# Two decoder blocks on one core: the turning of seven norms spread into the products around them

## What is computed

```python
def rms_norm(x, g):          # the seven norms before mlp, gate, mixers
    y = x * rsqrt(mean(x * x, axis=-1) + 1e-6)
    return y * g

h = h + mixer(rms_norm(h, ln_mix)) @ w_out
h = h + square(relu(rms_norm(h, ln_mlp) @ w_mlp1)) @ w_mlp2
gate = sigmoid(rms_norm(h, ln_ple) @ w_ple_gate)
h = h + (p @ w_ple_proj) * gate
...
x = x + rms_norm(y, post_norm)   # second decoder, y the mixer's output
```

## Time and profile before

| | us |
|---|---|
| median of 3 runs | 2127.03 (2123.44 to 2127.22) |
| the profiled execution | 2124.92 |
| its span, first to last instruction | 2123.1 |
| TensorE's matmuls busy in it | 2007.9 |
| DVE, ScalarE, GpSimd busy | 1068.2, 896.8, 221.3 |
| mean granted TensorE clock | 0.981 |

### The profile page before, as it was taken

One profiled execution on the slowest core, in us unless ns is written; L12 is line 12 of the kernel. 1 busy time (PEld: TensorE's weight loads), 2 busy tenths in 40 slices (PEclk: granted clock), 3 DMA queues, 4 the chain that ended last, 5 costly groups with the idle time before them and its releaser, 6 DMA issues. The chain is left out here.

```text
span 2123.1 us, 27350 instructions
## 1 busy us (share of the span) xinstructions
PE 2007.9 (95%) x11189; PEld 1614.4 (76%) x11189; DVE 1068.2 (50%) x1706; ACT 896.8 (42%) x1653; POOL 221.3 (10%) x225
## 2 busy tenths in 40 slices
PE   7999889999999899999999999998999899989888
PEld 6778768888887777557888888776887688856567
DVE  5676455343435442674543443446344655355763
ACT  5561354322314543674432232445334532245552
POOL 1020000000000000441000000000000034133440
PEclk9999999999999999999999999998999999999999
DMA  5221113332322123111223332122221156400001
GB/s 154 66 79 42 41 40 109 100 99 99 99 99 81 60 89 100 40 40 60 92 97 99 99 99 99 64 77 94 80 90 41 44 177 177 141 21 29 13 7 64
DMA packets 122481, 169.93 MB, mean 80 GB/s; under 512 B 7482, under 2 KB 83654, under 8 KB 122358
## 3 DMA queue, kind: packets, MB, share of 16 engines
q1 hardware_dynamic: 114502, 150.47, 21.9%
q0 software_dynamic: 5504, 14.58, 2.5%
q10 hardware_dynamic: 2352, 3.15, 0.4%
HBM read 158.22 MB, written 2.10 MB: 76 GB/s over the span
## 5 line engine op out<-in xcount | busy, mean ns | idle before, releaser
L412 DVE TENSOR_TENSOR WL<-RAW,WH 128x1024 fp32r<-128x1024 f32 (+1 forms) x283 | 347.7, 1231 | 376.8 <-ACT WH L482 376.3
L482 ACT CAST WH<-RAW 128x1024 fp32r<-128x1024 f32 (+1 forms) x283 | 293.3, 1038 | 392.8 <-PE PSUM L516 390.4
L516 PE MATMUL PSUM<-XH,WH 128*128 128x512 f32 (+4 forms) x1128 | 422.7, 375 | 7.9 <-DVE XL L412 3.8
L516 PE MATMUL PSUM<-XL,WH 128*128 128x512 f32 (+4 forms) x1128 | 414.8, 368 | 0.0
L516 PE MATMUL PSUM<-XH,WL 128*128 128x512 f32 (+4 forms) x1128 | 414.5, 367 | 0.0
L516 PE MATMUL PSUM<-WH,HP 128*128 128x512 f32 x1024 | 317.9, 390 | 1.9 <-DVE WL L412 1.9
L516 PE MATMUL PSUM<-WH,XH 128*128 128x512 f32 (+1 forms) x608 | 240.5, 396 | 16.6 <-DVE WL L412 10.4
L516 PEld LDWEIGHTS PSUM<-XH,WH 128*128 128x128 f32 (+3 forms) x1128 | 213.4, 189 | 47.1 <-DVE WL L412 4.9
L516 PEld LDWEIGHTS PSUM<-XL,WH 128*128 128x128 f32 (+3 forms) x1128 | 213.4, 189 | 36.8 <-issue 2.9
L516 PEld LDWEIGHTS PSUM<-XH,WL 128*128 128x128 f32 (+3 forms) x1128 | 212.9, 189 | 35.3
L516 PE MATMUL PSUM<-WL,XH 128*128 128x512 f32 (+1 forms) x608 | 233.0, 383 | 0.0
(11 more groups left out here) (236 smaller groups left out, 2489.9 us busy)
## 6 DMA issues: line engine op xcount, KB each, us to landing
RAW<-in_w_mlp_dram SPq DMA_DIRECT2D x64, 1024.0 KB, 5.2
RAW<-in_nsa_w_in_dram SPq DMA_DIRECT2D x14, 1024.0 KB, 5.5
RAW<-in_w_in_e_dram SPq DMA_DIRECT2D x12, 1024.0 KB, 5.3
RAW<-in_w_qkv_o_dram SPq DMA_DIRECT2D x12, 1024.0 KB, 5.2
RAW<-in_gla_w_in_dram SPq DMA_DIRECT2D x12, 1024.0 KB, 5.2
RAW<-in_w_ple_gate_dram SPq DMA_DIRECT2D x8, 1024.0 KB, 5.0
RAW<-in_w_out_e_dram SPq DMA_DIRECT2D x4, 1024.0 KB, 5.0
RAW<-in_w_out_o_dram SPq DMA_DIRECT2D x4, 1024.0 KB, 5.0
```

The costliest lines, as they stand in the source:

```text
L412: return x.do.tensor_tensor(o, a, b, op)
L482: a.do.copy(hi, r).then_inc(*up("w_hi", "w_hi", j))
L516: m = p.do.matmul(o, l, r, start=start and i == 0, stop=stop and i == len(pairs) - 1)
```

## The change

No instruction is added or dropped; the lists of TensorE, ScalarE and DVE are put in another order at seven norms.

- TensorE: in MLP0, MLP1, PLE0 and PLE1 the turns of tiles 0 to 2 stay, that of tile 3 goes behind the first half product (MLP), or behind two tiles of p's first product (PLE). In ODD and GLA tile 0's turn comes after tile 1's products, tile 1's inside tile 3 (after its first part of the tail), tiles 2 and 3 after the first and second half product. In NSA tiles 0 and 1 are both turned inside tile 3, tiles 2 and 3 as in ODD. `pe_turn` can take banks ahead of the ring.
- `dve_turn` is split into `dve_gain` and `dve_rest`, and the new lists `act_norm`, `dve_norm` (MLP and PLE norms) and the written-out ones of ODD, GLA and NSA interleave them with the scales, adds and weights of neighbouring tiles.
- TensorE waits for both halves of XL by name (`x_whole`), and `turns()` follows the new order.

```diff
 def out_norm(i, n):
-                for u in ([t - 1] if t else []) + ([3] if t == 3 else []):
+                for u in {2: (0, 1), 3: (2, 3)}.get(t, ()):
...
+        def x_whole(p, n, t):
+            for h in (1, 0):
+                p.wait_ge(*at("xl", n, t, h))
...
 def toks(...)
+                        if within and n > 1 and i == 0:
+                            within(t)
...
-        def pe_turn(p, n, t):
+        def pe_turn(p, n, t, ahead=None):
             for h in range(2):
                 p.wait_ge(*at("xn", n, t, h))
                 turned(p, ("nt", n, t, h), lambda b: [
...
-                    for c in range(4)])
+                    for c in range(4)], bank=None if ahead is None else (ps.next + ahead + h) % 8)
...
         def pe_ready(p, n, t):
             if t:
                 pe_turn(p, n, t - 1)
-            if t == 3:
-                pe_turn(p, n, 3)
...
+        def act_norm(a, n, j):
+            act_scale(a, n, 0)
+            act_scale(a, n, 1)
+            act_turn(a, n, 0)
+            act_scale(a, n, 2)
+            act_turn(a, n, 1)
+            act_weights(a, j + 2)
+            act_scale(a, n, 3)
+            act_weights(a, j + 3)
+            act_turn(a, n, 2)
+            act_turn(a, n, 3)
+
+        def dve_norm(v, n, j, add):
+            add(0)
+            dve_scale(v, n, 0)
+            add(1)
+            dve_gain(v, n, 0)
+            dve_scale(v, n, 1)
+            dve_rest(v, n, 0)
+            add(2)
+            dve_gain(v, n, 1)
+            dve_scale(v, n, 2)
+            dve_rest(v, n, 1)
+            dve_weights(v, j + 1)
+            add(3)
+            dve_weights(v, j + 2)
+            dve_scale(v, n, 3)
+            dve_gain(v, n, 2)
+            dve_rest(v, n, 2)
+            dve_weights(v, j + 3)
+            dve_gain(v, n, 3)
+            dve_rest(v, n, 3)
...
 def pe_mlp: up_
-                    feats_first(p, [("up", l, 0, m) for m in range(3)], n)
+                    feats_first(p, [("up", l, 0, m) for m in range(3)], n, mid=[lambda: pe_turn(p, n, 3)])
...
 def pe_ple
+            toks(p, ("pv", l, 0), p_ready, 1, "P", (PP[:, 0], PP[:, 1]), after=lambda t: pe_turn(p, n, 3) if t == 1 else None)
+            toks(p, ("pv", l, 1), p_ready, 1, "P", (PP[:, 0], PP[:, 1]))
             toks(p, ("pg", l, 0), normed(n), head=True)
-            toks(p, ("pg", l, 1), normed(n), tail=True, after=after)
+            toks(p, ("pg", l, 1), normed(n), tail=True, after=lambda t: pe_turn(p, n + 1, 0) if t == 1 else None,
+                 within=lambda t: pe_turn(p, n + 1, 1) if t == 3 else None)
...
 def act_ple, second column half of the gate
+            gate(1, 0)
+            act_scale(a, n + 1, 0)
+            gate(1, 1)
+            act_turn(a, n + 1, 0)
+            act_scale(a, n + 1, 1)
+            gate(1, 2)
+            act_weights(a, j + 4)
+            act_turn(a, n + 1, 1)
+            act_weights(a, j + 5)
+            gate(1, 3)
+            act_scale(a, n + 1, 2)
+            act_weights(a, j + 6)
+            act_scale(a, n + 1, 3)
+            act_turn(a, n + 1, 2)
+            act_turn(a, n + 1, 3)
...
 def dve_ple, second column half
+            add(1, 0)
+            dve_scale(v, n + 1, 0)
+            dve_gain(v, n + 1, 0)
+            add(1, 1)
+            dve_scale(v, n + 1, 1)
+            dve_rest(v, n + 1, 0)
+            dve_gain(v, n + 1, 1)
+            dve_weights(v, j + 4)
+            dve_rest(v, n + 1, 1)
+            add(1, 2)
+            add(1, 3)
+            dve_scale(v, n + 1, 2)
+            dve_weights(v, j + 5)
+            dve_gain(v, n + 1, 2)
+            dve_scale(v, n + 1, 3)
+            dve_weights(v, j + 6)
+            dve_rest(v, n + 1, 2)
+            dve_gain(v, n + 1, 3)
+            dve_rest(v, n + 1, 3)
...
 def pe_odd (pe_gla alike)
+            feats_first(p, [("oq", *f) for f in o_feats[:3]], ODD, mid=[lambda: pe_turn(p, ODD, 2, 0), lambda: pe_turn(p, ODD, 3, 2)])
...
 def pe_gla
+            def within(t):
+                if t == 3:
+                    pe_turn(p, NSA, 0)
+                    pe_turn(p, NSA, 1)
+            toks(p, ("yo", 0, 1), gla_ready, tail=True, within=within)
...
 def act_gla
+            out_scale(0)
+            out_scale(1)
+            act_scale(a, NSA, 0)
+            act_scale(a, NSA, 1)
+            out_scale(2)
+            act_turn(a, NSA, 0)
+            act_turn(a, NSA, 1)
+            act_weights(a, j + 4)
+            out_scale(3)
+            act_weights(a, j + 5)
+            act_scale(a, NSA, 2)
+            act_weights(a, j + 6)
+            act_scale(a, NSA, 3)
+            act_turn(a, NSA, 2)
+            act_turn(a, NSA, 3)
...
 def dve_gla
+            dve_out_gain(v, 0, 1, 0)
+            dve_out_add(v, 0, 0)
+            dve_out_gain(v, 0, 1, 1)
+            dve_out_add(v, 0, 1)
+            dve_scale(v, NSA, 0)
+            dve_out_gain(v, 0, 1, 2)
+            dve_scale(v, NSA, 1)
+            dve_gain(v, NSA, 0)
+            dve_gain(v, NSA, 1)
+            dve_out_add(v, 0, 2)
+            dve_rest(v, NSA, 0)
+            dve_rest(v, NSA, 1)
+            dve_weights(v, j + 4)
+            dve_out_gain(v, 0, 1, 3)
+            dve_out_add(v, 0, 3)
+            dve_scale(v, NSA, 2)
+            dve_weights(v, j + 6)
+            dve_gain(v, NSA, 2)
+            dve_scale(v, NSA, 3)
+            dve_rest(v, NSA, 2)
+            dve_gain(v, NSA, 3)
+            dve_rest(v, NSA, 3)
...
 def pe_nsa
+            feats_first(p, [("ns",), ("nq", 0), ("nq", 1)], NSA, "SFF", [lambda: pe_turn(p, NSA, 2), lambda: pe_turn(p, NSA, 3)])
```

More of the change, by code:

```diff
@@ L851, in down, with add @@
                 dve_weights(v, j + (3 if q == 3 and c else 5))
-                for t in range(4):
+                def add(t):
                     o = H[:, t, 512 * c:512 * c + 512]
@@ L855, in down @@
                     tt(v, o, o, bank("down", l, q, c, t)[:, :], ALU.add).then_inc(*ps.read("down", l, q, c, t))
+                if q == 3 and c:
+                    dve_norm(v, n + 1, j + 3, add)
+                    return
+                for t in range(4):
+                    add(t)
                     if q == 3:
[L857 to L860, removed]
+                        dve_half(v, n + 1, t)
                 if q < 3 or c == 0:
@@ L907, in act_ple, with gate @@
                 act_weights(a, first_part["pv", l, c] + 3)
[L908 to L927, removed]
+            def gate(c, t):
+                g = GTE[:, t, 512 * c:512 * c + 512]
+                a.wait_ge(*ps.full("pg", l, c, t))
+                act(a, g, bank("pg", l, c, t)[:, :], ACT.Exp, scale=-1.0).then_inc(*ps.read("pg", l, c, t))
+                a.wait_ge(*ps.free("pg", l, c, t))
+                step(a, act(a, g, g, ACT.Ln, bias=ONEC))
+                act(a, g, g, ACT.Exp, scale=-1.0).then_inc(*up("ple_gate", "ple_gate", l, c, t))
+            j = first_part["pg", l, 0]
+            act_weights(a, j + 5)
+            for t in range(4):
+                gate(0, t)
+                if t:
+                    act_half(a, n + 1, t - 1)
+            act_half(a, n + 1, 3)
+            act_weights(a, j + 6)
+            j = first_part["pg", l, 1]
+            act_weights(a, j + 3)
+            gate(1, 0)
[13 more added lines that the diff above has]
+            act_turn(a, n + 1, 3)
         def dve_ple(v, l):
@@ new lines, in dve_ple @@
+            j = first_part["pg", l, 0]
+            dve_weights(v, j + 5)
+            for t in range(4):
+                add(0, t)
+                if t:
+                    dve_half(v, n + 1, t - 1)
+            dve_half(v, n + 1, 3)
+            dve_weights(v, j + 6)
+            j = first_part["pg", l, 1]
+            dve_weights(v, j + 3)
+            add(1, 0)
[3 more added lines that the diff above has]
+            dve_scale(v, n + 1, 1)
@@ L1723, in round_ @@
                     pv(h)
-            feats_first(p, [("oq", *f) for f in o_feats[:3]], ODD)
+            feats_first(p, [("oq", *f) for f in o_feats[:3]], ODD, mid=[lambda: pe_turn(p, ODD, 2, 0), lambda: pe_turn(p, ODD, 3, 2)])
             for k in range(8):
@@ L1828, in act_odd @@
             act_weights(a, j + 3)
-            for t in range(4):
-                act_ready(a, MLP1, t, j + 3)
+            act_norm(a, MLP1, j + 3)
         def dve_odd(v):
@@ L1915, in dve_odd @@
                     tt(v, o, o, bank("oo", c, t)[:, :], ALU.add).then_inc(*ps.read("oo", c, t))
-                    if c:
-                        dve_ready(v, MLP1, t, j + 3)
-                    else:
+                if c:
+                    dve_norm(v, MLP1, j + 3, add)
+                else:
+                    for t in range(4):
+                        add(t)
                         dve_half(v, MLP1, t)
-                if not c:
                     dve_weights(v, j + 6)
```

123 lines of the change are left out of this document (41 added, 82 removed).

## The result

The changed kernel takes 2098.98 us (median of 4, 2096.64 to 2099.40) against 2125.59 (median of 4, 2123.44 to 2127.22) of the kernel before in the same session: a ratio of 0.9873, 95% interval 0.9856 to 0.9890, some 27 us. The profiled execution took 2099.40 with a span of 2097.2; the span before was 2123.1.

A forecast was written before the change was run, and what follows sets the result against it. TensorE, busy 95% of the span, was taken as the bound. Gains of 2.9 + 4.8 + 3.4 + 5.95 + 5.7 + 7.3 = 30.0 us took 2124.92 to 2094.9; 2.1 for the median gave 2097, range 2089 to 2110.

The forecast's parts named there:

- What bounds: Whole kernel: TensorE binds; at seven norms 33.8 us of XN waits and 14.2 us of low-clock loss.
- MLP1, PLE0, PLE1: Tile 3's turn hidden behind product work at these norms: gains of 2.9, 2.4 and 2.4 us.
- the 0.6 us wait for WL: MLP1's first half product: TensorE waits 0.6 us for the first new weights, instead of 2.03 us at the turn.
- The bank wait foretold at PLE: PLE0 and PLE1: p's second half waits near 0.7 us for its bank, which DVE copies after tile 3's rest.
- MLP0: MLP0 norm: a gain of 3.4 us, with only two parts (2.7 us) covering each tile.
- the term of 2.4 us for the first weight: MLP0: the first weights are there 2.4 us after TensorE has run out of work.
- the 0.7 for a low clock: MLP0: 0.7 us taken off for an even chance that low clock (1.5 us) follows the weight wait.
- ODD and GLA: These two norms: gains of 5.95 and 5.7 us, after new waits of 2.8 and 2.7 us.
- NSA: NSA norm: a gain of 7.3 us, after new waits of 1.3, 3.4 and 0.6 and 1.0 for the clock.
- The GpSimd term: NSA: GpSimd's rests and DVE's work go one after the other, 1.5 us at the first product, 0.5 before second halves.
- the rivals: Whole kernel: queues take half back, 2111, chance 0.14; low clock stays, 2106, 0.10; slower, 0.04; does nothing, 2127, 0.02.
- The rival "slower": First weight work before add 3 or gate 3 waits for its transfer and delays the add; 2131.4 or more, chance 0.04.

The follow-up runs named there:

- the run with filled waits: The kernel before, no turn moved, with 17 to 56 transposes that nobody reads in each of TensorE's waits at the norms: 2117.39 us.
- the banks mended: The changed kernel with tile 2's turn in MLP1 given a bank other than the one holding tile 3's product: 2090.31 us.
- The undone halves: The changed kernel, in MLP and PLE norms, with ScalarE's and DVE's old order (2109.56 us), or with tile 3's turn ahead of the first products again (2113.56 us).
- The later turn: The changed kernel with tile 0's turn in ODD and GLA within tile 2's product instead of ahead of it: 2098.40 us.
- The five runs with banks: The changed kernel with NSA banks 2088.14, MLP1 banks 2090.31, both 2087.87, ring set ahead of nz 0 2093.50; the kernel before with that ring line 2122.81 us.
- the old lists: The changed kernel with ScalarE's and DVE's lists in the MLP and PLE norms back in their old order: 2109.56 us.
- two programs: The changed kernel with all bank edits and NSA's low halves on DVE: 2080.91 us; the same plus 26 unread transposes before NSA's first product: 2085.28 us.

## Why the prediction was right, and where it was not

The time was forecast at 2097 and is 2098.98; the range holds it. The gain was forecast at 30.0 us and is 26.6 by the medians of one session, 25.9 in the traces. That it is so near is in part luck, since errors met: the seven norms gave 2.6 more than foretold and other places 2.4, and 9.2 were lost where the prediction did not look.

- **What bounds**: right. The XN waits fell from 33.8 to 7.2 us (7 expected), and the run with filled waits shows the clock's part to be real, at 11.4 us of the 14.2 claimed (one of NSA's waits stayed unfilled).
- **MLP1, PLE0, PLE1**: 2.4, 2.6, 2.6 for 2.9, 2.4, 2.4. In MLP1 the 0.6 us wait for WL did not come; a bank wait of 1.17 came in its place (with the banks mended the wait for WL is there, 0.43). The sum took the weights as the only thing that could hold TensorE and did not follow the ring. The bank wait foretold at PLE is there and smaller (0.36 for 0.6). The undone halves show that turns and lists are both needed.
- **MLP0**: the term of 2.4 us for the first weight was wrong. TensorE waited 0.79 us there, for XL. DVE had split two weight tiles in one go at 296.18, as it had at 296.38 in the kernel before; the tail uses up only two parts, so one of the first product's weights was ready long before. The row was there to read, and the sum had gone by the rule of the other norms. With the 0.7 for a low clock that did not follow, that makes 2.3 of the 2.6 us missed.
- **ODD and GLA**: the waits came at the places and sizes foretold: 1.56 and 1.53 for 1.5, 0.61 for 0.7, 0.32 and 1.23 for 0.6 and 1.2. ODD got 0.9 more, since the low clock that had followed a wait for weights near 720 was absent. The later turn shows that the 1.5 us are not the turn's fault, which the sum had charged to it.
- **NSA**: 1.00 for 1.3, 3.23 for 3.4, 0.24 for 0.6; 6.5 us for 7.3, since the low clock behind the 3.23 cost more than 1.0 (6.8 us of it). The GpSimd term was of the right kind: in NSA DVE's sum of 1024 columns and its two subtractions took 1.2 us more beside GpSimd at the first product, for the 1.5 of the sum. The page "SBUF — State Buffer" of the Trainium skill, section "SBUF: two separate sides", has the pair of ports locked for the whole of an instruction. The trace agrees: DVE's first subtraction, begun at 1662.83, took 1.75 us, until 0.54 behind the end of GpSimd's at 1664.03, and the next took its usual 0.68.
- **What the sum lacked**: the 9.2 us behind NSA, more than any term of the sum was off. "No product, transpose or DMA is added or removed; everything is moved" was the sentence that failed: a turn that is moved takes its bank at another point of the ring, and every product behind it, 150 us on, lies on another bank. Neither the sum nor a rival has this; the rivals looked for waits on data only. The five runs with banks show it. The rival "slower" did not come: no add waited for a weight's transfer.

The page "TensorE: Matmul & The Clock Gate" of the Trainium skill, section "What's actually happening", says the number of slow matmuls varies from run to run and should not be fitted. The runs of one kernel agree (2104.71 to 2110.40 with the old lists, at mean clocks of 0.988 to 0.990), and from trace to trace the stretches at 236, 712 and 2025 us are there or not (1.6, 1.6 and 2.7 us). The same section puts the penalty under 1% of a typical span. The 11.4 us are 0.5% of this one, which agrees, and yet they are as much as four tenths of what the change gained.

## What to carry to other kernels

When work is moved between buffers handed out in turn, write down the buffer of every later user before and after, and look for pairs where the old content is read late; here one index was worth 10.8 us, four tenths of what the whole change gained. Undo each half of a change that spans several engines: of 13.6 us the turns alone kept 5.2 and the lists alone 1.4, by the start times of the same products; the medians, which hold the scatter of the whole kernel, would have said 3.0 and nothing. And before a wait is charged to the instruction that waits, ask which engine binds that stretch; if it is another one, moving the waiter gains nothing.

## What the runs showed of the hardware that was not expected

The same wait does not always have the same price: 1.42, 2.57 or 2.8 us of idle time are followed by 3.4, 3.4 and 6.8 us at half clock in one program and by none in another, with identical instructions there. That parts the medians of two programs by up to 4 us (2080.91 and 2085.28) with nothing to show for it at the edit, as much as many single edits are worth; only the landmarks told the two apart. And GpSimd loses with DVE: of its two subtractions of 512 columns in the NSA norm (3.50 us together) the first took 1.30 us and the second, begun at 1661.79 beside DVE's sum of 1661.49 to 1662.90, took 2.23.
